# State-space layer: the convolution's first tap, with its bias, moved from VectorE to ScalarE

## What is computed

```python
zxbcdt = h @ w_in
z, xbc, dt = jnp.split(zxbcdt, [SSD_D_INNER, SSD_D_INNER + SSD_CONV_DIM], axis=-1)
xbc = jax.nn.silu(causal_depthwise_conv_2(xbc, conv_w, conv_b))   # 4 taps over time, plus bias
xs, b_in, c_in = jnp.split(xbc, ...)
...
cb = jnp.einsum('bclgn,bcsgn->bcgls', c_c, b_c)
y_diag = jnp.einsum('bcgjls,bcsgjp->bclgjp', cb[:, :, :, None] * decay, xdt)
states = jnp.einsum('bclgn,bclgjp->bcgjpn', b_c, xdt * decay_to_end[..., None])
...
y = y + xs.astype(f32) * jnp.repeat(d_skip.astype(f32), SSD_HEAD_DIM)
g = (y * jax.nn.silu(z.astype(f32))).reshape(...)
g = g * lax.rsqrt(jnp.mean(g * g, axis=-1, keepdims=True) + EPS)
```

## Time and profile before

| | |
|---|---|
| median of 3 runs | 2621.29 us (2621.23 to 2623.13) |
| profiled execution | 2620.9 us, span 2619.1 us, mean granted clock 0.994 |
| PE busy | 2538.4 us, 97% |
| PE weight loads | 2171.7 us, 83% |
| VectorE busy | 1166.5 us, 45% |
| ScalarE busy | 976.9 us, 37% |
| GpSimd busy | 1020.9 us, 39% |
| state-space stage | about 1055 to 1500 us of the span |

### The profile page before, as it was taken

The page is one execution under the profiler, slowest core; times in us unless marked ns, Lnnn a source line. Parts: engine busy times, 40 slices in busy tenths (PEclk is TensorE's granted clock), DMA queues, the critical chain, the costliest instruction groups (busy, mean ns, idle before and its releaser), DMA issues. The chain is left out here.

```text
span 2619.1 us, 36294 instructions
## 1 busy us (share of the span) xinstructions
PE 2538.4 (97%) x15064; PEld 2171.7 (83%) x15064; DVE 1166.5 (45%) x1672; ACT 976.9 (37%) x1490; POOL 1020.9 (39%) x759
## 2 busy tenths in 40 slices
PE   7999999999999999799999899999999999999999
PEld 5777777777777787799999899999996666788887
DVE  6454452165445423689899533111235554412211
ACT  4333333343333334345444433222335554423321
POOL 4444444334444443233333245444433010544443
PEclk9999999999999999899999999999999999999999
DMA  4233233223323322112222133223222000233232
GB/s 142 91 101 107 90 95 97 88 75 104 104 91 101 105 84 71 57 57 66 73 58 65 50 96 97 89 89 91 88 75 73 17 25 17 89 105 97 89 97 89
DMA packets 61268, 215.55 MB, mean 82 GB/s; under 512 B 8176, under 2 KB 8560, under 8 KB 61104
## 3 DMA queue, kind: packets, MB, share of 16 engines
q1 hardware_dynamic: 57248, 202.05, 25.8%
q10 hardware_dynamic: 3856, 11.18, 1.3%
HBM read 211.10 MB, written 2.10 MB: 81 GB/s over the span
## 5 line engine op out<-in xcount | busy, mean ns | idle before, releaser
L368 POOL TENSOR_TENSOR sb_w_lo<-sb_w_raw,sb_w_hi 128x512 fp32r<-128x512 f32 x754 | 1019.8, 1375 | 1575.3 <-ACT sb_w_hi L1163 1575.1
L395 PE MATMUL psum<-sb_h_hi,sb_w_hi 128*128 128x512 f32 (+1 forms) x2648 | 813.2, 348 | 31.0 <-DVE sb_h_lo L1678 21.2
L395 PE MATMUL psum<-sb_h_lo,sb_w_hi 128*128 128x512 f32 (+1 forms) x2648 | 791.9, 340 | 0.0
L395 PE MATMUL psum<-sb_h_hi,sb_w_lo 128*128 128x512 f32 (+1 forms) x2648 | 788.8, 339 | 0.0
L1163 ACT ACTIVATE sb_w_hi<-sb_w_raw 128x1024 fp32r<-128x1024 f32 x377 | 395.7, 1054 | 627.9 <-PE psum L395 457.6
L395 PEld LDWEIGHTS psum<-sb_h_hi,sb_w_hi 128*128 128x128 f32 x2648 | 456.3, 189 | 103.2 <-issue 26.2
L395 PEld LDWEIGHTS psum<-sb_h_lo,sb_w_hi 128*128 128x128 f32 x2648 | 455.4, 189 | 59.7 <-issue 3.8
L395 PEld LDWEIGHTS psum<-sb_h_hi,sb_w_lo 128*128 128x128 f32 x2648 | 455.4, 189 | 55.9
L395 PE MATMUL psum<-sb_mix_hi,sb_w_hi 128*128 128x264 f32 (+1 forms) x1424 | 415.5, 337 | 13.9 <-POOL sb_w_lo L368 5.8
L395 PE MATMUL psum<-sb_mix_lo,sb_w_hi 128*128 128x264 f32 (+1 forms) x1424 | 410.9, 334 | 0.0
L395 PE MATMUL psum<-sb_mix_hi,sb_w_lo 128*128 128x264 f32 (+1 forms) x1424 | 409.5, 333 | 0.0
(11 more groups left out here) (290 smaller groups left out, 2334.2 us busy)
## 6 DMA issues: line engine op xcount, KB each, us to landing
sb_w_raw<-in_weights SPq DMA_DIRECT2D x377, 512.0 KB, 3.5
sb_decay<-in_decay ACTq DMA_DIRECT2D x16, 640.0 KB, 3.8
sb_resid<-in_x SPq DMA_DIRECT2D x4, 512.0 KB, 8.9
out<-sb_resid SPq DMA_DIRECT2D x8, 256.0 KB, 2.1
sb_s<-in_positions ACTq DMA_DIRECT2D x1, 256.0 KB, 7.7
sb_cols<-in_cols ACTq DMA_DIRECT2D x1, 158.5 KB, 4.9
sb_table<-in_rope_table ACTq DMA_DIRECT2D x1, 132.0 KB, 3.2
sb_ones<-in_ones ACTq DMA_DIRECT2D x1, 64.0 KB, 5.9
```

The source lines that it names most:

```text
L368: low = e.tensor_tensor(g.w_lo[:, u % 4, at], g.w_raw[:, u % 2, at], g.w_hi[:, u % 4, at].bitcast(F32), ALU.subtract)
L395: mm = e.matmul(g.psum[0:m, at + b, 0:wd], w[:, slot, P * i:P * i + m], xs[:, tile, c:c + wd], start=first and n == 0, stop=last and n == 2)
```

## The change

ScalarE computes the first tap with the bias as an Identity activation whose scale is the tap's weight and whose bias is the convolution's bias, both one value per partition. It signals "first_tap", for which VectorE's first remaining tap waits. VectorE keeps three taps, now in one piece for channel 1 too. On ScalarE the tap of channel h of the next group stands after the Exps of head h (at h = 1 after the Ln and two Exps) and ahead of the split; in the opening the taps alternate with the silus.

```diff
+def act_ssd_silu(g, e, grp, i):
+    S = g.S
+    t = ssd_channels(g, grp, i)
+    e.wait_ge(S["conv2"], 4 * grp + i + 1)
+    e.activation(t, t, ACT.Silu).then_inc(S["silu"], 1)
...
@@ act_ssd
-    act_ssd_silus(g, e, 0)
+    for i in range(4):
+        act_ssd_first_tap(g, e, 0, i)
+        if i >= 1:
+            act_ssd_silu(g, e, 0, i - 1)
+    act_ssd_silu(g, e, 0, 3)
     act_split(g, e, U_SSD + 2 + LEAD)
...
                 act_ssd_decays_from_start(g, e, grp, 1)
+            if grp < GROUPS - 1:
+                act_ssd_first_tap(g, e, grp + 1, h)
             if h and (grp < GROUPS - 1 or h < HG - 1):
                 act_split(g, e, U_SSD + GROUP * (grp + 1) + h + LEAD)
...
+def act_ssd_first_tap(g, e, grp, i):
+    S = g.S
+    ch, n = ssd_conv_channel(grp, i), 4 * grp + i + 1
+    if i == 0 and grp:
+        e.wait_ge(S["cb_sum"], grp)
+    if i == 1 and grp >= 2:
+        e.wait_ge(S["c_state"], 2 * (grp - 1))
+    e.wait_ge(S["dt_v"], 1)
+    e.wait_ge(S["lifted"], n)
+    e.activation(ssd_channels(g, grp, i), g.lift[:, i % 2, 3:3 + L], ACT.Identity, bias=g.col("ssd_bias", ch),
+                 scale=g.col("ssd_conv", 4 * ch + 3)).then_inc(S["first_tap"], 1)
...
-def dve_ssd_conv(g, e, grp, i, parts=range(4)):
+def dve_ssd_conv(g, e, grp, i):
...
-    for part in parts:
-        if part == 0:
...
-            e.tensor_scalar(out, g.lift[:, i % 2, 3:3 + L], g.col("ssd_conv", 4 * ch + 3),
-                            g.col("ssd_bias", ch), ALU.mult, ALU.add).then_inc(S["tap2"], 1)
+    for part in range(1, 4):
+        if part == 1:
+            e.wait_ge(S["first_tap"], n)
         else:
-            e.wait_ge(S["tap2"], 3 * n - 3 + part)
...
+            e.wait_ge(S["tap2"], 2 * n - 3 + part)
...
@@ dve_ssd
             if h == 1:
-                if not last:
-                    dve_ssd_conv(g, e, grp + 1, 1, range(0, 1))
                 dve_ssd_weights(g, e, grp, 2)
-                if not last:
-                    dve_ssd_conv(g, e, grp + 1, 1, range(1, 2))
                 dve_ssd_state_y(g, e, grp, 1)
...
             if not last:
-                dve_ssd_conv(g, e, grp + 1, h, range(2 if h == 1 else 0, 4))
+                dve_ssd_conv(g, e, grp + 1, h)
```

More of the change, by code:

```diff
@@ L114 @@
     "dt_scaled", "dt_a", "dt_v", "dt_turned", "dt_end", "lifted", "z_in", "z2",
-    "tap2", "conv2", "silu", "b_turned", "bt2", "cb_sum", "cb", "x_turned", "xdt", "states_sum",
+    "first_tap", "tap2", "conv2", "silu", "b_turned", "bt2", "cb_sum", "cb", "x_turned", "xdt", "states_sum",
     "state", "a_row", "decay1", "masked", "decay2", "c_state", "state_y", "with_skip", "first_skip", "weighted", "y_part", "skip", "gated", "y_sq", "y_sq_sum",
@@ L1285, in ssd_channels @@
     return (g.bt[:, :], g.ct[:, grp % 2, :], g.xs[:, 2 * grp, :], g.xs[:, 2 * grp + 1, :])[i]
+def act_ssd_silu(g, e, grp, i):
[3 more added lines that the diff above has]
+    e.activation(t, t, ACT.Silu).then_inc(S["silu"], 1)
 def act_ssd_silus(g, e, grp):
     S = g.S
[L1291 to L1295, removed]
+    for c in range(2):
+        z = g.zs[:, 2 * (grp - 1) + c, :]
+        e.wait_ge(S["z_in"], 2 * (grp - 1) + c + 1)
+        e.activation(z, z, ACT.Silu).then_inc(S["z2"], 1)
     if grp < GROUPS:
         for i in range(4):
-            t = ssd_channels(g, grp, i)
-            e.wait_ge(S["conv2"], 4 * grp + i + 1)
-            e.activation(t, t, ACT.Silu).then_inc(S["silu"], 1)
+            act_ssd_silu(g, e, grp, i)
 def act_ssd_squares(g, e, grp):
@@ L2016, in dve_ssd_gate, with ssd_conv_channel @@
                     ALU.mult).then_inc(S["z_in"], 1)
-def dve_ssd_conv(g, e, grp, i, parts=range(4)):
+def ssd_conv_channel(grp, i):
+    return (16 + grp, 24 + grp, 2 * grp, 2 * grp + 1)[i]
+def act_ssd_first_tap(g, e, grp, i):
     S = g.S
-    ch = (16 + grp, 24 + grp, 2 * grp, 2 * grp + 1)[i]
-    out, n = ssd_channels(g, grp, i), 4 * grp + i + 1
-    for part in parts:
-        if part == 0:
[L2026 to L2031, removed]
-            e.tensor_scalar(out, g.lift[:, i % 2, 3:3 + L], g.col("ssd_conv", 4 * ch + 3),
-                            g.col("ssd_bias", ch), ALU.mult, ALU.add).then_inc(S["tap2"], 1)
-        else:
-            e.wait_ge(S["tap2"], 3 * n - 3 + part)
-            mm = e.scalar_tensor_tensor(out, g.lift[:, i % 2, 3 - part:3 - part + L],
-                                        g.col("ssd_conv", 4 * ch + 3 - part), out, ALU.mult, ALU.add)
-            mm.then_inc(S["tap2" if part < 3 else "conv2"], 1)
+    ch, n = ssd_conv_channel(grp, i), 4 * grp + i + 1
[9 more added lines that the diff above has]
+    S = g.S
+    ch, n = ssd_conv_channel(grp, i), 4 * grp + i + 1
+    out = ssd_channels(g, grp, i)
+    for part in range(1, 4):
+        if part == 1:
+            e.wait_ge(S["first_tap"], n)
+        else:
+            e.wait_ge(S["tap2"], 2 * n - 3 + part)
+        mm = e.scalar_tensor_tensor(out, g.lift[:, i % 2, 3 - part:3 - part + L],
+                                    g.col("ssd_conv", 4 * ch + 3 - part), out, ALU.mult, ALU.add)
+        mm.then_inc(S["tap2" if part < 3 else "conv2"], 1)
 def dve_ssd_xdt(g, e, grp, c):
```

## The result

The changed kernel takes 2655.11 us (median of 4 runs, 2654.37 to 2657.72) against 2622.21 us for the kernel before (2621.23 to 2623.81): a ratio of 1.0127, 95% interval 1.0111 to 1.0142. It is 33 us slower; 20.6 were forecast. The profiled execution has a span of 2652.6 us against 2619.1.

What follows compares the result with a forecast made beforehand. PE was taken to bound the kernel, so added PE waits are lost one for one. 6 x 3.6 + 1.3 - 2.3 = +20.6 us on 2620.9, with the median 0.4 above, gave 2642; range from 3 below 2631 to 2660.

Steps and rivals of the forecast that it cites:

- What bounds the kernel: State-space stage: PE, busy 48.62 of 49.30 us a group, sets the end; VectorE and ScalarE matter only where PE waits.
- The opening, -2.3: Opening of the stage: PE's first wait shrinks by 0.6, its second by 2.35 us; -2.3 us in all.
- the bound of -4.9: Opening: low end if the clock holds behind PE's second wait, at most 2.6 us more gain.
- The relay: Steady groups: splits and Exps queue behind the waiting tap; 24.3 us from pair product to turning of B, against 20.5 of work.
- The size per group, +3.6: Groups 1 to 6: +3.8 at the turning of B, +0.2 handoffs, -0.4 gate wait; +3.6 us each, 2.5 to 5.7.
- the weight supply is not hurt: Steady groups: a split delayed by six microseconds still has two units of PE, over ten microseconds, ahead of its use.
- The gate's gain: Steady groups: PE's wait for the gate, 0.4 us a group, goes away because VectorE is idle when it falls due.
- Group 0, +1.3: First group: no copies (1.2) and no low parts (1.3), so only +1.3 us, between 0 and 3.
- rival 2: Groups: the clock falls in every one behind waits of about 2 us, 2.6 us more each; 2660 or 2667; chance 0.06.
- Rival 1: Groups: VectorE's relief counts, the order on ScalarE does not, so only gains stay; 2614 to 2617; chance 0.11.
- Rival 3: Taps among the Exps: each Identity costs table load and reload, 2 x 1.28; 45 us over seven groups, 2687; chance 0.03.

Runs made afterwards that it cites:

- e1: Kernel before, all taps on VectorE, plus ScalarE waiting for each channel's lift where the change puts the tap; 2646.58 us, ratio 1.0092.
- e5: Changed kernel with tap 0 in place, taps 1 and 2 behind the Exps of heads 2 and 3, tap 3 between the silus; 2624.87 us, ratio 1.0014.
- e7: Changed kernel with the squares of the group before put ahead of the setup's second weight split; 2649.46 us, ratio 1.0106.
- e9: Changed kernel with only taps 1 and 2 of the groups on ScalarE, one step later, taps 0 and 3 on VectorE, opening kept; 2624.74 us, ratio 1.0006.
- e2: Changed kernel with each step's weight split ahead of the tap instead of behind it; 2663.32 us, ratio 1.0155.
- e3: Changed kernel with all group taps one step later on ScalarE, behind the next head's Exps, the last between the silus; 2656.78 us, ratio 1.0134.
- e6: Changed kernel with tap 3 alone moved to between the silus; 2659.14 us, ratio 1.0144.

## Why the prediction was right, and where it was short

**What bounds the kernel: right.** PE sets the end, and VectorE's relief bought nothing in the groups. VectorE's busy time fell by 38.9 us (1166.5 to 1127.6) and not only by the 19 of the taps; some steps that met GpSimd before met it no more, such as the norm's step, 0.71 instead of 1.68. No run counts these out.

**The opening, -2.3: right, a little more.** The first wait shrank by 0.6 as summed, the second by 2.1; to the turning of x it is 3.2 in all, 0.9 more than forecast. The waits account for 2.7. The clock fell less behind the second wait (from there to the turning of x 6.0 us instead of 6.9), as the bound of -4.9 had allowed for, and more ahead of it, which took 0.4 back.

**The relay: right, link by link.** From the end of the first pair product, forecast and measured in the group shown: lift of channel 1 after 1.4 and 1.5, Exps of head 2 after 5.7 and 5.8, lift of channel 2 after 10.5 and 10.7, Exps of head 3 after 13.6 and 13.9, lift of channel 3 after 19.5 and 19.9, silu of B after 24.3 and 24.8. The tap takes 0.83 (0.82 forecast), and the collision with GpSimd at the weighting of head 3 costs 1.09 (1.79 against 0.70; 1.07 forecast). The forecast waits came at the named places, with VectorE idle 4.3 and 3.2 (some 4 and 3 forecast). e1 and e5 together show that the place makes the loss: the wait there costs 24.3 us of the groups' 34.3 with no tap on ScalarE (e1), and all the taps in other places cost none (e5). The tap's own length counts only where it stands in the relay.

**The size per group, +3.6: too small.** An undisturbed group lost 5.0 (54.3 from turning to turning, 1254.03 to 1308.34, against 49.35). Of the 1.4 missing, 0.3 is the relay's (its handoffs from VectorE to ScalarE took 0.09 to 0.12, not 0.03) and about 0.9 is a term that was left out: the wait for xdt, behind "the weight supply is not hurt". No weight came late for PE, but the second split of the setup waited for its DMA, and the squares and with them VectorE stood behind it. e7 shows that the wait goes when the squares stand ahead of the split. The gate's gain is as forecast.

**Group 0, +1.3: wrong by size.** It lost 4.1. It has no copies and no low parts, as summed, but the weighting of head 2 also ran into GpSimd, which it escapes in the later groups, where the copies stand between the split and the Exps (0.76 in the group shown):

```profile
1126.22 1.82 DVE L2114 TENSOR_TENSOR sb_part<-sb_part,sb_cbd 88x528 f32<-88x528 f32 x1 [3.22 <-ACT sb_part L1356]
...
1135.41 1.79 DVE L2114 TENSOR_TENSOR sb_part<-sb_part,sb_cbd 88x528 f32<-88x528 f32 x1 [3.22 <-ACT sb_part L1356]
```

1.82 and 1.79 instead of 0.70 each. The clock fell in this group as well.

**The clock, rival 2 at 0.06: in part it came, and not at its price.** I had it fall in all groups or in none. It fell in three of seven, behind waits of 2.4 us that left it at 1.00 in the other four. PE's busy time rose by 8.0 us, but next to nothing of it reached the end of the group: the three groups with a fall lost about what the others did, where I had put 2.6 us more on each, as the relay and not PE set when the next step could start. The terms as measured give 6 x 5.0 + 4.1 - 3.2 = 31, against 33.5 in the spans and 33 in the medians; the remaining 2.5 lie ahead of the stage.

**Rival 1** (ScalarE's idle time absorbs the taps) fell for the change as written, and e5 and e9 show what it would have taken: another place for three taps of four. **Rival 3** (table loads) fell: no load stands at the tap's line, and ScalarE has 1522 instructions against 1490, 32 more for 32 taps. The Trainium skill, "ScalarE: Activation LUTs", "Table sets: the hidden batching unit", says that identity is in every set; the trace agrees for the sets used here.

## What to carry to other kernels

A step moved to an idle engine is paid for by what is queued behind it, not by its own length: write down what it waits for, when that is ready, and which later instruction of the same queue another engine is waiting for. Here taps of 0.83 us, each waiting ahead of the next Exps of 1.4 us, cost 5 us a group, and with three of the four put one place later they cost nothing. Before you move a second step to mend it, look at which other engine's work or which DMA its earlier start will meet: e2 took 2.9 us out of the chain and put some 4.5 in.

## What the runs showed that I had not expected

- Earlier splits on ScalarE lengthened VectorE's work through GpSimd: three taps of 128x528 took 2.4 us beside an idle GpSimd and 3.3 to 4.3 beside its subtractions (e2, e3, e5), and in e2 the kernel became 8 us slower. The Trainium skill, "SBUF — State Buffer", "SBUF: two separate sides", describes such a lock between the two, with the loser blocked; a loss of 0.8 to 1.1 for each meeting is what the rows show, against 1.25 for one GpSimd step.
- The same wait of PE, 2.35 to 2.4 us, was followed by a full clock in some groups of a run and by a fall to 0.71 and 0.61 in others; the 2.9 us waits of e3 were followed by one in six groups of seven. A wait's length alone did not tell in these traces whether the clock would fall.
- A clock fall has no fixed price. In e2 the period was 56.0 us with or without one, since a later wait of PE shrank by what the fall took; in e3, where no such wait followed, a group with a fall lost 1.0 to 2.2 us more than the one without (group 0 apart).
- Two waits at different instructions can be two ends of one late relay: with one cut, e6 showed the other at its full length and an unchanged period.
